# Activation tiles at another start address, and norm row sums in column groups

## The reference, cut to what matters

```python
def rms_norm(t, w):
    y = t * lax.rsqrt(jnp.mean(t * t, axis=-1, keepdims=True) + NORM_EPS)
    return y * w
...
h = modulate(rms_norm(x, mix_norm[layer]), sh1, sc1)
y = mixer(h, ...)
x = x + g1[:, None, :] * y
h = modulate(rms_norm(x, ffn_norm[layer]), sh2, sc2)
x = x + g2[:, None, :] * swiglu(h, ffn_w1[layer], ffn_w2[layer])
```

## Time and profile before

| | |
|---|---|
| time, median of 3 runs | 3362.37 us (3358.93 to 3364.56) |
| the profiled execution | 3360.01 us, of which the span from first to last instruction is 3358.3 us |
| TensorE busy | 3254.2 us, 97%, 14052 matmul records |
| VectorE, ScalarE, GpSimd busy | 1968.4 us, 1145.1 us, 103.6 us |
| DMA | 370.04 MB, 110 GB/s on the mean |
| granted TensorE clock, mean | 0.989 of 2.4 GHz |

### The profile page before, as it was taken

How to read it: one execution, slowest core, us unless ns; L and a number is a source line. 1 busy time by engine, 2 the same in 40 slices (tenths; PEclk the granted TensorE clock), 3 DMA queues, 4 the chain that set the end, 5 groups by cost and what they waited for, 6 DMA issues and landing times. The chain is left out here.

```text
span 3358.3 us, 39117 instructions
## 1 busy us (share of the span) xinstructions
PE 3254.2 (97%) x14052; PEld 2500.2 (74%) x14052; DVE 1968.4 (59%) x2761; ACT 1145.1 (34%) x1545; POOL 103.6 (3%) x172
## 2 busy tenths in 40 slices
PE   5999999998899999999999999999999999999999
PEld 2446788886678888767888876688887758888887
DVE  7885765535668864566766367676645554455523
ACT  3324422224632222444433221443333353252222
POOL 1000011000001000000000010000000100000000
PEclk9998999999999999999999999999999999999999
DMA  8222455541125543212222335222233222222222
GB/s 302 90 69 82 136 200 193 164 137 63 50 95 197 191 154 93 83 44 82 88 100 92 97 100 137 68 87 100 91 97 132 75 75 82 95 87 96 98 95 88
DMA packets 105053, 370.04 MB, mean 110 GB/s; under 512 B 11664, under 2 KB 11664, under 8 KB 104688
## 3 DMA queue, kind: packets, MB, share of 16 engines
q1 hardware_dynamic: 83696, 289.02, 26.3%
q0 software_dynamic: 20096, 75.38, 6.7%
q10 hardware_dynamic: 1152, 4.19, 0.3%
HBM read 357.80 MB, written 2.10 MB: 107 GB/s over the span
## 5 line engine op out<-in xcount | busy, mean ns | idle before, releaser
L2417 DVE TENSOR_TENSOR weight_lo<-weight_ring,weight_hi 128x1024 fp32r<-128x1024 f32 (+1 forms) x473 | 571.6, 1209 | 914.7 <-ACT weight_hi L1666 907.3
L1666 ACT ACTIVATE weight_hi<-weight_ring 128x1024 fp32r<-128x1024 f32 (+1 forms) x473 | 494.5, 1046 | 1599.4 <-PE proj_banks L939 972.2
L939 PE MATMUL proj_banks<-h_lo,weight_hi 128*128 128x512 f32 x1672 | 650.5, 389 | 0.0
L939 PE MATMUL proj_banks<-h_hi,weight_hi 128*128 128x512 f32 x1312 | 510.5, 389 | 0.5 <-DVE weight_lo L2417 0.5
L939 PE MATMUL proj_banks<-h_hi,weight_lo 128*128 128x512 f32 x1312 | 510.4, 389 | 0.0
L939 PEld LDWEIGHTS proj_banks<-h_lo,weight_hi 128*128 128x128 f32 x1672 | 313.9, 188 | 65.2
L939 PEld LDWEIGHTS proj_banks<-h_hi,weight_hi 128*128 128x128 f32 x1312 | 246.3, 188 | 51.8 <-issue 0.8
L939 PEld LDWEIGHTS proj_banks<-h_hi,weight_lo 128*128 128x128 f32 x1312 | 246.3, 188 | 51.0
L939 PE MATMUL proj_banks<-mid_hi,weight_hi 128*128 128x512 f32 x704 | 273.9, 389 | 0.0
L939 PE MATMUL proj_banks<-mid_lo,weight_hi 128*128 128x512 f32 x704 | 273.9, 389 | 0.0
L939 PE MATMUL proj_banks<-mid_hi,weight_lo 128*128 128x512 f32 x704 | 273.9, 389 | 0.0
(11 more groups left out here) (428 smaller groups left out, 5161.2 us busy)
## 6 DMA issues: line engine op xcount, KB each, us to landing
weight_ring<-in_w_up SPq DMA_DIRECT2D x176, 512.0 KB, 3.3
ada_ring<-in_ada POOLq DMA_DIRECT2D x96, 512.0 KB, 3.7
weight_ring<-in_w_dn SPq DMA_DIRECT2D x64, 512.0 KB, 3.5
weight_ring<-in_w_br SPq DMA_DIRECT2D x32, 512.0 KB, 3.2
weight_ring<-in_w_upr SPq DMA_DIRECT2D x32, 512.0 KB, 3.3
weight_ring<-in_w_dnr SPq DMA_DIRECT2D x32, 512.0 KB, 3.3
weight_ring<-in_w_dn SPq DMA_DIRECT2D x32, 384.0 KB, 3.1
cond<-in_ada POOLq DMA_DIRECT2D x20, 512.0 KB, 4.6
```

Source lines behind the costliest of these rows:

```text
L939: last = mm(proj.banks[:, u % RING, :], stationary(home + n)[:, w], moving(k), start=k + m == 0, stop=k == kt - 1 and m == 2)
L1666: return nc.scalar.activation(out, in_, func, **kw)
L2417: return v.tensor_tensor(out, a, b, op)
```

## The change

The first part moves four small tiles (`m_bias`, `gain`, `ada_acc`, `small`) from behind the scratch area to before it and puts 32 unused bytes (`between`) after them, 1216 bytes together. Everything from h on then begins 64 bytes behind a multiple of 256 (h at byte 75072, the scratch tiles at 91456). x, the weight ring, its two parts, and the modulation ring that lies under `late_rounded` are allocated earlier and stay at 128. In a split product the one operand now begins at 64 and the other at 128, but where the activation is in `late_rounded` (the last block's feed-forward, line 939 from 3015 us on, and part of its branches) both stay at 128.

The second part lets `row_sums` use the constant `pick_wide` (four blocks of 128 x 32, block j with a one in column j), and each token block writes to 32 PSUM partitions of its own, so that the sums of block j end in row 33j of a 128-row tile. Root and reciprocal run on 128 partitions, and `spread_rows` picks row 33j by a column of a new constant, repeated 128 times as weights.

```diff
+        "own_row": np.eye(P)[:, 0:P:33],
...
         self.late_r = sb("late_rounded", [P, (ADA_RING + 1) * D], F32R)
+        self.m_bias = sb("m_bias", [4, 2])
+        self.gain = sb("gain", [P, 9 * 8])
+        self.acc = sb("ada_acc", [P, 8])
+        self.small = sb("small", [P, 208])
+        sb("between", [P, 8])
         with ExitStack() as mixing:
...
-        self.m_bias = sb("m_bias", [4, 2])
         self.mod = sb("mod", [P, 4 * 48])
-        self.gain = sb("gain", [P, 9 * 8])
-        self.acc = sb("ada_acc", [P, 8])
-        self.small = sb("small", [P, 208])
...
-        bank = (open_bank(mix, ("ss", r)) if first else mix.bank(("ss", r)))[0:4, 0:P]
+        bank = open_bank(mix, ("ss", r)) if first else mix.bank(("ss", r))
         for j in range(NB):
-            ins = mm(bank, c.const("pick")[:, 4 * j:4 * j + 4], squares[:, j * P:(j + 1) * P], start=first and j == 0,
-                     stop=last and j == NB - 1)
+            ins = mm(bank[32 * j:32 * j + 32, 0:P], c.const("pick_wide")[:, 32 * j:32 * j + 32], squares[:, j * P:(j + 1) * P], start=first, stop=last,
+                     skip_group_check=True)
...
-            last = mm(bank[:, j * P:(j + 1) * P], c.const("sel")[0:4, j * P:(j + 1) * P], T(RSTD)[0:4, at * P:(at + 1) * P], start=True, stop=True)
+            row = c.const("own_row")[:, j:j + 1].broadcast_to([P, P])
+            last = mm(bank[:, j * P:(j + 1) * P], row, T(RSTD)[:, at * P:(at + 1) * P], start=True, stop=True)
...
-        ins = f(T(RSTD)[0:4, 0:P], mix.bank(("ss", r))[0:4, 0:P], ACT.Sqrt, scale=1.0 / D, bias=eps[0:4, :])
+        ins = f(T(RSTD)[:, 0:P], mix.bank(("ss", r))[:, 0:P], ACT.Sqrt, scale=1.0 / D, bias=eps)
...
-        st.done(v.reciprocal(T(RSTD)[0:4, P:2 * P], T(RSTD)[0:4, 0:P]), s["rstd_ready"])
+        st.done(v.reciprocal(T(RSTD)[:, P:2 * P], T(RSTD)[:, 0:P]), s["rstd_ready"])
```

More of the change, by code:

```diff
@@ L1782, in final_norms @@
         act.wait_ge(s["final_sum"], 1)
-        both = T(RSTD)[0:4, 2 * P:3 * P]
-        f(both, both, ACT.Sqrt, scale=1.0 / D, bias=c.const("eps_squared")[0:4, :]).then_inc(s["final_sum"], 1)
-        f(T(RSTD)[0:4, 0:P], mix.bank(("ss", 8))[0:4, 0:P], ACT.Sqrt, scale=1.0 / D, bias=eps[0:4, :]).then_inc(mix.emptied(("ss", 8))[0], 1)
+        both = T(RSTD)[:, 2 * P:3 * P]
+        f(both, both, ACT.Sqrt, scale=1.0 / D, bias=c.const("eps_squared")).then_inc(s["final_sum"], 1)
+        f(T(RSTD)[:, 0:P], mix.bank(("ss", 8))[:, 0:P], ACT.Sqrt, scale=1.0 / D, bias=eps).then_inc(mix.emptied(("ss", 8))[0], 1)
         shift_and_round(9)
@@ L3154, in final_norms @@
     def final_norms():
-        both = T(RSTD)[0:4, 2 * P:3 * P]
+        both = T(RSTD)[:, 2 * P:3 * P]
         dve.wait_ge(*mix.filled(("ss", 9)))
-        st.link(ts(both, mix.bank(("ss", 8))[0:4, 0:P], EPS, ALU.mult))
-        tt(both, both, mix.bank(("ss", 9))[0:4, 0:P], ALU.add).then_inc(s["final_sum"], 1)
+        st.link(ts(both, mix.bank(("ss", 8))[:, 0:P], EPS, ALU.mult))
+        tt(both, both, mix.bank(("ss", 9))[:, 0:P], ALU.add).then_inc(s["final_sum"], 1)
         dve.wait_ge(s["final_sum"], 2)
         dve.sem_inc(*mix_release(mix, ("ss", 9)))
-        st.done(v.reciprocal(T(RSTD)[0:4, 3 * P:4 * P], both), s["rstd_ready"])
+        st.done(v.reciprocal(T(RSTD)[:, 3 * P:4 * P], both), s["rstd_ready"])
         dve.wait_ge(*mix.emptied(("ss", 8)))
-        st.done(v.reciprocal(T(RSTD)[0:4, P:2 * P], T(RSTD)[0:4, 0:P]), s["rstd_ready"])
+        st.done(v.reciprocal(T(RSTD)[:, P:2 * P], T(RSTD)[:, 0:P]), s["rstd_ready"])
         scale_tiles(9)
```

## The result

The changed kernel takes 3407.56 us (median of 4 runs, 3406.69 to 3410.07) against 3360.65 us for the kernel before (4 runs, 3358.18 to 3364.56): a ratio of 1.014, with a 95% interval of 1.0126 to 1.0154. It is 47 us slower, where 119 us less were forecast. Its profiled execution took 3407.27 us, of which the span is 3405.6 us.

A forecast was written before the change was run, and what follows sets the result against it. TensorE's start-to-start matmul distance was taken as the bound. Savings of 99.5 (split products), 7.8 (token stages) and 11.5 us (norms), together 118.8 off 3360.0, gave 3241.2, forecast as 3244 us; range 3230 to 3302 us.

The forecast's parts named there:

- The step that failed: Split products: moving the two operands' reads 64 bytes apart brings 9128 matmuls to at best 215.8 ns, saving 99.5 us.
- the 10.9 ns between float32r and plain float32: Per float32r matmul: extra gap, 13.3 against 2.5 ns, put down to reading the moving operand while loading weights.
- Rival C: Split products outside the last feed-forward part: 64 bytes apart is worse, 122 us more, 3473 us in all; chance 0.16.
- Rival A: All float32r matmuls: the 13.3 ns has nothing to do with addresses, only the norms gain, 3351 us; chance 0.31.
- The token stages: 1440 matmuls with operand roles exchanged, sign of the 64 bytes unknown: half of 15.7 us, a 7.8 us saving.
- The last feed-forward part: 720 records: two thirds, those reading late_rounded, should keep 226.7 ns, separating the two reads from the whole program.
- A fixed extra: Each float32r matmul was said to pay 13.3 ns over its pass, whatever its length.
- The norms: Row sums in column groups: 7.6 us at norms 1 to 7, 1.3 at norm 0, 2.6 at joined ones, 11.5 saved.
- Rival D: Norms' column groups don't overlap, bound by loads of 32 columns, and matmul distance stays: 3362 us; chance 0.03.
- The path: Whole span: the saving stays on TensorE's path; VectorE at 59% and ScalarE at 34% don't become the bound.

The follow-up runs named there:

- m2_streams: Small kernel without the computation, only float32r matmuls, varying lengths, address distances and one operand held at a single column: 215.8 ns per matmul with the moving operand held.
- m3_loads: Small kernel without the computation, float32r matmuls of 512 columns with fewer loaded columns or partitions: 231.3 ns with 32 loaded columns at equal start addresses modulo 256.
- e1_align_only: Kernel before with only the four small tiles moved, norms' code as it was: 3422.39 us against 3360.84 us, ratio 1.0178.
- m1_residues: Small kernel without the computation, float32r matmuls over 64 pairs of start addresses modulo 256: of 512 columns, 227 ns at equal ones, 229 to 234 ns at others.
- e4_weights_64: Changed kernel with weights and modulation ring at 64 and activations at 128: 3379.81 us against 3360.69 us for the kernel before, ratio 1.0056.
- m4_pairs: Small kernel without the computation, groups of 48 float32r matmuls whose start addresses change between matmuls: 231.7 ns with own pair equal, 233.1 ns with next load equal.
- e2_norms_only: Changed kernel with all tiles at their former addresses, so only the norms' code is new: 3349.54 us, ratio 0.9964 to the kernel before.

## Why the prediction was wrong

- **The step that failed** is "equal residues are the case in which they meet most", and with it the value for the first part, -99.5 us. The bound it was built on can be reached: the 10.9 ns between float32r and plain float32 vanish when the moving operand stands still (215.8 ns in m2_streams). But moving the operands apart doesn't make them vanish. Of all differences tried, none of the 512-column groups with a running moving operand settled under 226 ns; the kernel before stood at the best one. That two reads meet in the memory, which the step took as the cause, no run shows: a quarter of the load cost no less (m3_loads). In the changed kernel the loops went to 232.9 ns.
- **Rival C was the right case, with its term too large.** It was priced at 13.4 ns for each of 9128 matmuls; e1_align_only measures 61.6 us for the first part, or 61.6 / 9128 = 6.7 ns if all is put on them. It was to decide from 1.3 ns on, and it did. The argument against it was the failed step once more. Its own mechanism, reads that take turns, no run shows.
- **Rival A fell** in m1_residues: the distance does go by the addresses, from 227 to 234 ns with the same number of columns loaded. The Trainium skill (TensorE: Matmul & The Clock Gate, "Step-by-step: what each phase is for") has two independent ports and a load that takes no read bandwidth from the running matmul. What the prediction drew from it, an unmoved distance, didn't come true for float32r; the ports themselves no run shows. The 215.8 ns between starts of the Trainium skill (same page, "Back-to-back issue gap") were met by float32r of 512 columns in m2_streams, where the moving operand was a single column, and not where it ran through the memory. For plain float32 the prediction's agreement with it isn't exact: two such gaps are 431.7 ns by estimate, and 429.2 were measured.
- **The token stages** were put at -7.8 us, as half of a gain, with the sign left open. They are at +64 and have 2.0 ns more for each of 1440 matmuls by the starts above, +2.9 us. That the sign matters was named as unknown and is shown by e4_weights_64.
- **The last feed-forward part** was to keep two thirds of its matmuls at 226.7 ns. Its mean, 228.9 ns, is what that gives with the other third at 233.5, but the reason is wrong: the three products have 229.3, 229.2 and 228.3 ns. In e4_weights_64 the rule by shares fails by 4.4 ns, and in m4_pairs by 4.3.
- **A fixed extra** of 13.3 ns "whatever its length" was read from two lengths, 512 and 256 columns. At equal residues 448 columns took 206.5 ns in m2_streams, 19.8 over the 186.7 of one pass at 2.4 GHz.
- **The norms** were right term by term: 1.08 us at a middle norm, 1.3 at norm 0, 2.5 for 2.6 at the joined ones. In all 11.5 us were forecast and e2_norms_only measured 11.3, with 8 to 16 us as its interval. Rival D, that the groups don't overlap, fell with it.
- **The path** was right: VectorE and ScalarE became no bound, and the added matmul time shows in the end. By the starts the split products have 62 us more; less 11.3 us that is 51 us, and 47 were measured, with 42 to 52 us as the interval, so that the 4 us between can't be told from the spread.

## What to carry to other kernels

Before moving a tile that float32r matmuls of 512 columns read, write down where both operands of the hottest ones begin modulo 256, and keep the difference if it is zero: here it was worth 62 us of 3361, while the norms' column groups without the move were a plain gain to 3349.5 us. A residual cost that is the same in every stage may already be the lowest of the variable it hides; where the trace has only one value of that variable, both signs are open, and a small kernel that sweeps it answers it at once. Row sums of few columns, written in column groups of 32, run side by side: 0.57 us for two sets where it was 1.84.

## What the runs showed of the hardware that was not expected

- The distance between float32r matmuls of 512 columns that load 128 neighbouring columns depends on the sequence of start addresses modulo 256: 226.7 ns at equal ones, 229 to 234 at other steps of 32 bytes, 215.8 when the moving operand is a single column.
- Equal residues aren't the best at every length. In m2_streams 448 columns took 206.5 ns at equal residues, 202.2 at -64 and 200.0 at +64; 320 columns took 146.6 to 146.8 at all three.
- The means of m2_streams' groups of 128 and 192 columns don't compare by residue: at equal residues they are 182.5 and 215.5 ns, at -64 113.0 and 112.9, but the granted clock was not the same. At equal residues it fell to 0.50 in the group of 128 columns, behind a group of 64 columns at 1.00, and came back to 1.00 in the group of 256, which took 213 ns for each matmul before that and 120 after. The first row below is the group of 192 columns at equal residues, the second those of 128 to 256 columns at -64 (stretch, length, busy time of TensorE, weight loads, ScalarE and GpSimd, granted clock, DMA share and GB/s).

```profile
164.00:169.30 5.30, 5.30 (x26) 5.30 (x26) 0.00 (x0) 0.00 (x0) 0.50 0.00 0
189.00:196.00 7.00, 7.00 (x64) 7.00 (x64) 0.00 (x0) 0.00 (x0) 1.00 0.00 0
```

- In m3_loads the groups with 32 partitions took 426.7 ns for each matmul (lines 68 and 69 above), which is 512 columns at 1.2 GHz: the granted clock is 0.50 there, and 1.00 while the groups with 64 partitions ran just before. The stretches of that kernel, in the same columns:

```profile
119.00:136.00 17.00, 17.00 (x75) 13.19 (x73) 0.00 (x0) 0.00 (x0) 1.00 0.00 1
145.00:165.00 20.00, 20.00 (x48) 14.73 (x46) 0.00 (x0) 0.00 (x0) 0.50 0.00 0
```
